# Four residual norms: the first two tiles prepared in token halves, and every residual add moved from GpSimd to VectorE

## The chip, the cores and the metric

The kernel runs on one core of a Trainium2 chip. The metric is the device time of one launch in microseconds (us), lower is better. Engines are named by the profile's short names: PE is TensorE (matmuls), DVE is VectorE, ACT is ScalarE, POOL is GpSimd, SP is the engine whose queue issues the weight loads.

## The reference, cut to what matters

512 tokens of width 1024, all in float32, go through a first block (dilated and stick-breaking attention, cross attention, a gated MLP) and then through a second block of two layers. In that second block every sub-layer ends with a norm of its output that is added onto the residual, and the next sub-layer begins with a norm of the new residual:

```
h = h + 0.5 * rms_norm_2(swiglu(rms_norm_2(h, g[0]), ...), g[1])   # "post" norm g[1] onto h
hn = rms_norm_2(h, g[2])                                           # "pre" norm of the sum
m = gmlp_mixer(hn, ...)            # layer 0;   layer 1: rwkv7_mixer(hn, ...)
h = h + rms_norm_2(m, g[3])
h = h + 0.5 * rms_norm_2(swiglu(rms_norm_2(h, g[4]), ...), g[5])
gate = sigmoid(rms_norm_2(h, g[6]) @ ple_w_gate[i])
h = h + rms_norm_2(gate * (p[i] @ ple_w_proj[i]), g[7])
```

where `rms_norm_2(x, g) = x * rsqrt(mean(x*x) + 1e-6) * g`.

## The kernel before, in words

The residual `h` and the outputs lie feature-major in SBUF: 8 tiles of 128 features x 512 tokens. A matmul in float32 accuracy is made of three products on operands rounded to a shorter type: high x high, high x low and low x high, where high is the rounded value and low the rest. So ACT makes `xh` (high) and DVE makes `xl` (low) of each activation tile, and ACT and DVE split each chunk of weights into `wh` and `wl` (L329 and L345). Weight chunks stream from HBM in a fixed order, two ahead, each issued by SP when the `wl` of the chunk two before is made. Engines run their queues in program order and meet by counting semaphores; no planner is at work, the order is that of the Python text.

The change concerns the class `Deferred`, the stage at the boundary of two sub-layers, where it has a post norm to be added onto `h`. Steps at such a boundary:

1. PE sums the squares of the sub-layer's output (L824), ACT takes the root (L787), DVE the reciprocal (L879), and PE spreads the result over the partitions by four small matmuls into PSUM, one for each block of 128 tokens (L854, in the order 0, 2, 1, 3, with one wait in the middle). PE then multiplies a constant with no use for the result (`keep_busy`, L1000), 5 matmuls long.
2. For each tile t, DVE multiplies the output by gain and scale into a scratch tile (`gained`, L929); the scratch has two buffers. The sum onto `h` is made by DVE for tile 0 (`add_first`, L940) and by POOL for tiles 1 to 7 (`add_on_pool`, L936).
3. For each tile, ACT makes the high part of `h` times the next norm's gain (L1062), and DVE the low part (`low`, L1115). The scale of the next norm is not in it: it is applied to the products later, at the eviction.
4. PE multiplies each tile as it arrives against the first two chunks of weights (`multiply_arriving`): high with `wh` and with `wl` for the first chunk, high with `wh` for the second, then, at tile t, it waits for the low part of tile t itself.
5. Only after its own tiles does DVE split the next weight chunk (L345), add up the 7 squares that ACT makes of `h` (L874), and, ahead of a feed-forward, form sums and differences of `h` (`mixed_first`, `mixed_rest`, L2538 to L2549). PE sums the squares (L817) after three quarters of the second chunk's `wl` products; ACT and DVE make the scale (L883 to L887), PE spreads it (L858) within the third chunk's products.

Boundaries with such a post norm are six. Two of them (class `Beside`, before the gate of the embedding) have other matmuls woven in. The other four lie ahead of the gated mixer's first matmul (`gv`, from 1240 us on) and ahead of three feed-forwards (from 1530, 1947 and 2772 us on). Ahead of the feed-forwards a matmul moves 512 tokens; in `gv` the tokens are the stationary side, 4 blocks of 128, and a matmul has 256 columns of weights.

Of the kernel before, what the change touches and what calls it, by code (L numbers as in the profile page):

```python
# [233 lines left out]
def _build(nc, io, ctx, block):  # L234
# [113 lines left out]
    def linear(name, kt, cols, xs, act_part=None, dve_part=None, steps=(0, 0), halves=False, token_blocks=None,  # L348
# [152 lines left out]
        def _(pe):  # L501
            def multiply(unit, half, m, t, fresh, only=None):


                slot, lot = (a + unit // lots * per + half) % 2, unit % lots
                b, o = bank(unit, m)
                hi, lo = xs(t + half * kt)
                r = last_rows if t == kt - 1 else P
                if token_blocks:
                    wc, xc = slice(t * cols, (t + 1) * cols), slice(token_blocks[m] * P, (token_blocks[m] + 1) * P)  # L510
                    products = [(hi[0:r, xc], wh[0:r, slot, wc]), (hi[0:r, xc], wl[0:r, slot, wc]),
                                (lo[0:r, xc], wh[0:r, slot, wc])]
                    out = ps[:, b, o:o + cols]
                else:
# [4 lines left out]
                    hi, lo = hi[:, tokens], lo[:, tokens]  # L519
                    products = [(wh[0:r, slot, wc], hi[0:r]), (wh[0:r, slot, wc], lo[0:r]),  # L520
                                (wl[0:r, slot, wc], hi[0:r])]
                    out = ps[0:mc, b, 0:hi.shape[-1]]
# [18 lines left out]
            def multiply_arriving():  # L541
# [26 lines left out]
                last.then_inc(chunks_used, 1)  # L568

            def multiply_by_halves(unit, opened):  # L570

# [23 lines left out]
            if paired:  # L595
                multiply_arriving()
                for unit in range(1, in_halves):
                    multiply_by_halves(unit, filled and unit == 1)
# [26 lines left out]
    class Stage:  # L625
# [27 lines left out]
        scaled_late = False  # L653
        tile_by_tile = False

        def sum_pe(self, pe):
# [8 lines left out]
    class Made(Stage):  # L665
# [3 lines left out]
        def __init__(self, per_tile):  # L669
            self.per_tile, self.base = per_tile, dve_steps.base  # L670
# [60 lines left out]
    class Pass:  # L731
# [3 lines left out]
        def __init__(self, number, source, gain, split=None, plain=None, onto=False, tokens=EVERY, by="tensor",  # L735
                     deferred=False, total=None, stat=0):
            self.source, self.gain, self.split, self.plain, self.onto, self.tokens = source, gain, split, plain, onto, tokens
# [14 lines left out]
            for s, n in ((n_square, 0 if by == "before" else KD), (n_add, KD - 1 if by == "vector" else 0),  # L752
                         (n_sum, KD if by == "tensor" else 1), (n_mean, 0 if self.quarters else 1), (n_root, 1),
                         (n_scale, 1 if self.quarters else 2), (n_spread, 4 if self.quarters else 1),
                         (n_value, 0 if deferred else KD), (n_onto, KD if onto else 0), (n_high, KD if split else 0),
                         (n_low, KD if split else 0)):
                self.at[s] = s.total
                s.total += n

        def wait(self, engine, s, step):  # L760

            engine.wait_ge(s.sem, self.at[s] + step)

        def view(self, x):
            return x.rearrange("p (a t) -> p a t", a=2) if self.quarters else x

        def wait_result(self, engine, t):

            self.wait(engine, n_onto if self.onto else n_low if self.split else n_value, t + 1)

# [140 lines left out]
        def dve(self, dve):  # L911
# [10 lines left out]
            self.finish(dve, KD - 1)  # L922

        def gained(self, dve, t):
            if t == 0:
# [7 lines left out]
        def add_on_pool(self, pool, t):  # L933
            self.wait(pool, n_value, t + 1)
            dst = h[:, t, self.tokens]
            nc.gpsimd.tensor_tensor(dst, self.scratch(2 + t % 2), dst, ALU.add).then_inc(n_onto.sem, 1)  # L936
# [65 lines left out]
    class Deferred(Stage):  # L1002

        scaled_late = True
        ahead = None


        def __init__(self, gain, post=None, source=None, split=x_split, tokens=EVERY, keep=None, summed_before=False,
# [6 lines left out]
            self.keep = rs if keep is None else keep  # L1015
            self.post = Pass(0, by="before", **post) if post else None
            self.two = Pass(1, self.source, gain, tokens=tokens, by="before" if summed_before else "vector", deferred=True,
# [3 lines left out]
            self.high_at, self.low_at, self.kept_at = n_high.total, n_low.total, n_kept.total  # L1021
            n_high.total += KD
            n_low.total += KD
# [6 lines left out]
        def split_act(self, act):  # L1030
# [13 lines left out]
            if not self.landed:  # L1044
                self.highs(act, 0, KD)
# [19 lines left out]
        def pe(self, pe):  # L1065
            if self.post:
# [6 lines left out]
                self.post.spread(pe)  # L1073
                keep_busy(pe, 5 if self.post.onto else 3)

# [4 lines left out]
        def split_dve(self, dve):  # L1080
# [8 lines left out]
            if self.post:  # L1089
                self.post.invert(dve)  # L1090
            for t in range(KD):
                if self.post and self.post.onto:
# [12 lines left out]
        def pool(self, pool):  # L1105
            if self.post and self.post.onto:
                for t in range(1, KD):
                    self.post.add_on_pool(pool, t)

        def low(self, dve, t):  # L1110
            if self.post:
                self.post.wait_result(dve, t)
            dve.wait_ge(n_high.sem, self.high_at + t + 1)
            hi, lo = self.split(t)
# [6 lines left out]
        def wait_high(self, pe, t):  # L1121
            pe.wait_ge(n_high.sem, self.high_at + t + 1)

        def squares_dve(self, dve):
# [1972 lines left out]
    class Beside(Deferred):  # L3097

        def __init__(self, gain, post):
            Deferred.__init__(self, gain, post=post)
# [1636 lines left out]
```

## Time and profile before

| | |
|---|---|
| time, median of 3 runs | 3203.94 us (3202.12 to 3207.87) |
| the profiled execution's own time | 3205.45 us |
| its span in the trace | 3203.6 us |
| mean granted PE clock | 0.997 |
| PE busy | 3143.8 us, 98% of the span |
| DVE busy | 2140.0 us, 67% |
| ACT busy | 1481.1 us, 46% |
| POOL busy | 127.4 us, 4% |

Busy time of an engine is the union of its instructions' times. Rows of the timeline below give: start in us from the span's start, duration in us, engine, line of the kernel, operation, output<-inputs, shape, count of instructions merged, and in brackets the idle time of that engine just before, with what ended it.

### The profile page before, as it was taken

To read this page: it belongs to the slowest core of one execution; us is meant where nothing else is said; L and a number is where in the kernel's file an instruction comes from. 1 tells how busy PE (TensorE), PEld (TensorE's weight loads), DVE (VectorE), ACT (ScalarE), POOL (GpSimd) and SP (SyncE) were. 2 spreads that over 40 slices of the span, in tenths; PEclk is the share of its full clock that TensorE was granted. 3 is DMA by queue.
4 is the path that set the end of the run, shared out by engine and by line. 5 is a ranking of instruction groups with operands and counts; after the bars stand their busy time and mean duration, and the time that the engine had idled before them with its cause. 6 is when DMAs were issued, how large, how long until landed. Compare 5 with 4: busy or idle time off the path is not lost. (4 is left out here: it accounts for less than half of the span.)

```text
span 3203.6 us, 54216 instructions
## 1 busy us (share of the span) xinstructions
PE 3143.8 (98%) x22914; PEld 2704.5 (84%) x22914; DVE 2140.0 (67%) x3130; ACT 1481.1 (46%) x2289; POOL 127.4 (4%) x131
## 2 busy tenths in 40 slices
PE   9999999999999999999999999999999999999998
PEld 7887787888889988988899887998777787799986
DVE  6546766775389845363898458996667665799737
ACT  3357644443255523432555345554336564455524
POOL 2100000000000001000100011000110000100002
PEclk9999999999999999999999999999999999999999
DMA  5311232232323323222232332332223000133331
GB/s 184 114 53 66 92 106 79 92 101 90 104 76 108 104 100 113 94 89 92 79 106 98 106 101 72 106 106 100 85 81 103 16 4 16 66 104 108 106 100 65
DMA packets 47249, 287.17 MB, mean 90 GB/s; under 512 B 6416, under 2 KB 6688, under 8 KB 21408
## 3 DMA queue, kind: packets, MB, share of 16 engines
q1 hardware_dynamic: 44960, 279.51, 25.7%
q0 software_dynamic: 2048, 4.20, 0.4%
q8 instruction: 182, 2.98, 0.4%
q14 instruction: 59, 0.48, 0.0%
HBM read 277.39 MB, written 2.10 MB: 87 GB/s over the span
## 5 line engine op out<-in xcount | busy, mean ns | idle before, releaser
L345 DVE TENSOR_TENSOR wl<-raw,wh 128x2048 fp32r<-128x2048 f32 (+3 forms) x211 | 424.8, 2013 | 324.1 <-ACT wh L329 323.6
L528 PE MATMUL ps<-xh,wh 128*128 128x512 f32 (+1 forms) x1312 | 511.4, 396 | 16.0 <-DVE wl L345 4.3
L528 PE MATMUL ps<-xl,wh 128*128 128x512 f32 (+1 forms) x1312 | 486.5, 391 | 0.3
L329 ACT CAST wh<-raw 128x2048 fp32r<-128x2048 f32 (+2 forms) x208 | 348.6, 1676 | 277.4 <-PE ps L528 267.6
L528 PE MATMUL ps<-xh,wl 128*128 128x512 f32 (+1 forms) x1312 | 462.0, 392 | 0.0
L2701 ACT CAST wh<-raw 128x512 fp32r<-128x512 f32 x432 | 262.5, 619 | 230.7 <-DVE raw L2720 114.4
L528 PE MATMUL ps<-hid_h,wh 128*128 128x512 f32 x880 | 342.8, 390 | 0.9 <-DVE wl L345 0.9
L528 PE MATMUL ps<-hid_l,wh 128*128 128x512 f32 x880 | 342.4, 389 | 0.0
L528 PE MATMUL ps<-hid_h,wl 128*128 128x512 f32 x880 | 342.3, 389 | 0.0
L2712 DVE TENSOR_TENSOR wl<-raw,wh 128x512 fp32r<-128x512 f32 x432 | 297.3, 690 | 65.3 <-ACT wh L2701 64.2
L2894 PE MATMUL ps<-mix_h,wh 128*128 128x256 f32 x1152 | 327.0, 284 | 1.3 <-DVE tmp L2831 1.2
L2895 PE MATMUL ps<-mix_l,wh 128*128 128x256 f32 x1152 | 326.0, 283 | 0.0
L2896 PE MATMUL ps<-mix_h,wl 128*128 128x256 f32 x1152 | 325.9, 283 | 0.0
L528 PEld LDWEIGHTS ps<-xh,wh 128*128 128x128 f32 (+1 forms) x1312 | 246.0, 188 | 84.3 <-issue 22.7
L528 PEld LDWEIGHTS ps<-xl,wh 128*128 128x128 f32 (+1 forms) x1312 | 245.6, 188 | 56.4 <-DVE xl L1115 2.9
L528 PEld LDWEIGHTS ps<-xh,wl 128*128 128x128 f32 (+1 forms) x1312 | 245.3, 187 | 53.3 <-issue 1.0
L2896 PE MATMUL ps<-xh,wl 128*128 128x256 f32 x864 | 244.5, 283 | 0.0
L2895 PE MATMUL ps<-xl,wh 128*128 128x256 f32 x864 | 244.5, 283 | 0.0
L2894 PE MATMUL ps<-xh,wh 128*128 128x256 f32 x864 | 244.5, 283 | 0.0
L2894 PEld LDWEIGHTS ps<-mix_h,wh 128*128 128x128 f32 x1152 | 221.1, 192 | 3.1 <-DVE tmp L2831 2.3
L2895 PEld LDWEIGHTS ps<-mix_l,wh 128*128 128x128 f32 x1152 | 221.1, 192 | 0.0
L2896 PEld LDWEIGHTS ps<-mix_h,wl 128*128 128x128 f32 x1152 | 221.1, 192 | 0.0
(537 smaller groups left out, 5918.2 us busy)
## 6 DMA issues: line engine op xcount, KB each, us to landing
raw<-in_up SPq DMA_DIRECT2D x88, 1024.0 KB, 4.9
raw<-in_down SPq DMA_DIRECT2D x64, 704.0 KB, 4.0
raw<-in_up_c SPq DMA_DIRECT2D x22, 1024.0 KB, 4.9
raw<-in_down_c SPq DMA_DIRECT2D x16, 704.0 KB, 4.0
raw<-in_gates SPq DMA_DIRECT2D x8, 1024.0 KB, 5.0
raw<-in_gv SPq DMA_DIRECT2D x8, 1024.0 KB, 4.9
raw<-in_gu SPq DMA_DIRECT2D x8, 1024.0 KB, 5.0
raw<-in_gout SPq DMA_DIRECT2D x8, 1024.0 KB, 4.8
```

Of the source, the lines that this page charges most:

```text
L329: nc.scalar.copy(wh[:, slot, 0:w], raw[:, slot, 0:w]).then_inc(hi_ready, 1)
L345: nc.vector.tensor_tensor(wl[:, slot, 0:w], raw[:, slot, 0:w], wh[:, slot, 0:w].bitcast(F32), ALU.subtract).then_inc(lo_ready, 1)
L528: last = nc.tensor.matmul(out, stationary, moving, start=(fresh and q == 0), stop=(t == kt - 1 and half == per - 1 and q == 2), skip_group ...
L2701: split = nc.scalar.copy(part(wh, u, what), source(u, what))
L2712: split = nc.vector.tensor_tensor(part(wl, u, what), source(u, what), part(wh, u, what).bitcast(F32), ALU.subtract)
L2894: nc.tensor.matmul(out, hi_w[:, at_], hi, start=(fresh and j == 0), stop=False, skip_group_check=True)
L2895: nc.tensor.matmul(out, hi_w[:, at_], lo, start=False, stop=False, skip_group_check=True)
L2896: done = nc.tensor.matmul(out, lo_w[:, at_], hi, start=False, stop=(j == KQ - 1), skip_group_check=True)
```

## The change

Four boundaries (all but the two of class `Beside`, which gets `whole = True`) are given a list `steps`: tile 0 and tile 1 for the first 256 tokens, tile 0 and tile 1 for the second 256 tokens, then tiles 2 to 7 whole. DVE scales and adds, ACT rounds, and PE multiplies in these ten steps. All adds onto `h` are on DVE. PE's order becomes: at tile t the high products of both chunks, then the low products of tile t-1 for both chunks. The spreading matmuls go in the order 0, 1, 2, 3 with two waits among them, and 2 `keep_busy` matmuls follow in place of 5.

```diff
+    def cut(x, part):
+        return x[:, part * (T // 2):(part + 1) * (T // 2)]
...
+            def multiply_arriving_halves():
+                pe.wait_ge(psum_read.sem, psum_read.base - 1)
+                pe.wait_ge(lo_ready, a + 1)
+                for t, part in norms.steps:
...
+                    opening = t == 0 and part == 0
+                    norms.wait_high_step(pe, t, part)
+                    for m in ms:
+                        fresh = opens(0, m, t) if token_blocks else opening
+                        multiply(0, 0, m, t, fresh, "high", part)
+                        multiply(0, 0, m, t, False, "weight_low", part)
...
+                    for m in ms:
+                        multiply(1, 0, m, t, opens(1, m, t) if token_blocks else opening, "high", part)
+                    if part != 0 and t:
+                        norms.wait_tile(pe, t - 1)
+                        for m in range(blocks):
+                            multiply(0, 0, m, t - 1, False, "x_low")
+                            multiply(1, 0, m, t - 1, False, "x_low")
+                norms.wait_tile(pe, kt - 1)
...
-                for n, b in enumerate((0, 2, 1, 3)):
-                    if n == 2:
-                        self.wait(pe, n_spread, 2)
+                for n, b in enumerate(range(TB) if self.halved else (0, 2, 1, 3)):
+                    if n in ((1, 3) if self.halved else (2,)):
+                        self.wait(pe, n_spread, n)
...
+        def gained_half(self, dve, t, part):
+            if t == 0:
+                self.wait(dve, n_spread, 2 + 2 * part)
+            nc.vector.scalar_tensor_tensor(cut(tmp[:, 2 + t, :], part), cut(self.source[:, t, :], part),
+                                           vec[:, self.gain + t:self.gain + t + 1],
+                                           ps[:, 2 + part, P:3 * P], ALU.mult, ALU.mult).then_inc(n_value.sem, 1)
+
+        def add_on_vector(self, dve, t, part):
+            self.wait(dve, n_value, self.done(t, part))
+            old, value = (x if part is None else cut(x, part) for x in (h[:, t, :], tmp[:, 2 + t % 2, :]))
+            nc.vector.tensor_tensor(old, value, old, ALU.add).then_inc(n_onto.sem, 1)
...
-                keep_busy(pe, 5 if self.post.onto else 3)
+                keep_busy(pe, 2 if self.steps else 5 if self.post.onto else 3)
...
+            if self.steps:
+                for t, part in self.steps[:4]:
+                    self.post.gained_half(dve, t, part)
+                    self.post.add_on_vector(dve, t, part)
+                self.post.gained(dve, 2)
+                self.low(dve, 0)
+                self.post.add_on_vector(dve, 2, None)
+                self.low(dve, 1)
+                for t in range(3, KD):
+                    self.post.gained(dve, t)
+                    self.post.add_on_vector(dve, t, None)
+                    self.low(dve, t - 1)
+                self.low(dve, KD - 1)
+                return
...
-                for t in range(1, KD):
+                for t in range(KD if self.steps else 1, KD):
                     self.post.add_on_pool(pool, t)
```

## Rows read from the trace of the kernel before

**Rows 1.** The page, busy time, share of span and instructions of each engine.

```profile
PE 3143.8 (98%) x22914; PEld 2704.5 (84%) x22914; DVE 2140.0 (67%) x3130; ACT 1481.1 (46%) x2289; POOL 127.4 (4%) x131
```

**Rows 2.** Timeline of PE at the boundary from 1947 us on.

```profile
1946.96 1.07 PE L854 MATMUL ps<-sums_p,const 32*128 32x128 f32 x8 [0.17 <-DVE sums_p L879]
1947.96 2.43 PE L1000 MATMUL ps<-const 128*128 128x256 f32 x10
1950.48 0.47 PE L528 MATMUL ps<-xh,wh 128*128 128x512 f32 x1
...
1969.43 2.88 PE L528 MATMUL ps<-xh,wl 128*128 128x512 f32 x12
1972.15 0.94 PE L817 MATMUL ps<-const,rs 128*128 128x1 f32 x8
...
1974.50 0.47 PE L528 MATMUL ps<-xh,wh 128*128 128x512 f32 x1 [0.37 <-ACT wh L329]
...
1977.49 1.12 PE L858 MATMUL ps<-rs,const 128*128 128x512 f32 x2 [0.44 <-DVE rs L887]
```

**Rows 3.** Waits of PE, whole span: us in total, times, longest.

```profile
PE ps L858 <- DVE rs L887: 1.3, 3, 0.5
```

**Rows 4.** Timeline of DVE at the same boundary.

```profile
1948.11 0.75 DVE L929 SCALAR_TENSOR_TENSOR tmp<-proj,vec,ps 128x512 f32<-128x512 f32 x1 [1.20 <-PE ps L854]
1948.89 0.69 DVE L940 TENSOR_TENSOR h<-tmp,h 128x512 f32<-128x512 f32 x1
1949.50 0.74 DVE L929 SCALAR_TENSOR_TENSOR tmp<-proj,vec,ps 128x512 f32<-128x512 f32 x1
...
1960.42 1.12 DVE L1115 SCALAR_TENSOR_TENSOR xl<-h,vec,xh 128x512 fp32r<-128x512 f32 x1
...
1963.56 0.75 DVE L1115 SCALAR_TENSOR_TENSOR xl<-h,vec,xh 128x512 fp32r<-128x512 f32 x1 [0.31 <-ACT xh L1062]
1964.23 2.28 DVE L345 TENSOR_TENSOR wl<-raw,wh 128x2048 fp32r<-128x2048 f32 x1
1966.43 5.46 DVE L874 TENSOR_TENSOR rs<-rs,tmp 128x512 f32<-128x512 f32 x7
...
1972.60 0.48 DVE L2546 SCALAR_TENSOR_TENSOR mix<-h,vec,mix 128x256 f32<-128x256 f32 x1
...
1976.74 0.69 DVE L887 TENSOR_TENSOR rs<-const,stats 128x512 f32<-128x512 f32 x1
```

**Rows 5.** Timeline of ACT at the same boundary.

```profile
1961.03 0.73 ACT L1062 ACTIVATE xh<-h,vec 128x512 fp32r<-128x512 f32 x1 [0.98 <-POOL h L936]
1962.73 0.72 ACT L1062 ACTIVATE xh<-h,vec 128x512 fp32r<-128x512 f32 x1 [0.98 <-POOL h L936]
...
1972.47 1.89 ACT L329 CAST wh<-raw 128x2048 fp32r<-128x2048 f32 x1
```

**Rows 6.** Timeline of POOL at the same boundary.

```profile
1950.32 1.29 POOL L936 TENSOR_TENSOR h<-tmp,h 128x512 f32<-128x512 f32 x1 [46.35 <-DVE tmp L929]
1952.89 9.80 POOL L936 TENSOR_TENSOR h<-tmp,h 128x512 f32<-128x512 f32 x6 [1.28 <-DVE tmp L929]
```

**Rows 7.** Lines L1062 and L3091, 256 columns: duration min/median/max, ns.

```profile
L1062 ACT ACTIVATE mem_h<-mem,vec x8: 496/498/507, 399.7 to 402.5; 128x256 fp32r<-128x256 f32 x8
...
L3091 DVE TENSOR_TENSOR proj<-tmp,proj x4: 418/419/420, 1943.2 to 3185.8; 128x256 f32<-128x256 f32 x4
```

**Rows 8.** Timeline of DVE and PE at the boundary of gv, from 1240 us.

```profile
1258.64 5.46 DVE L874 TENSOR_TENSOR rs<-rs,tmp 128x512 f32<-128x512 f32 x7
...
1262.46 3.04 PE L528 MATMUL ps<-wl,xh 128*128 128x256 f32 x24
...
1265.34 0.95 PE L817 MATMUL ps<-const,rs 128*128 128x1 f32 x8
```

**Rows 9.** Timeline of PE at 2368 us; then by windows (PEclk: third figure from the end).

```profile
2368.04 0.47 PE L528 MATMUL ps<-xh,wh 128*128 128x512 f32 x1 [1.89 <-DVE xl L3635]
...
2350.00:2375.00 25.00, 23.11 (x95) 17.24 (x94) 23.89 (x36) 13.18 (x18) 0.00 (x0) 0.93 0.26 85
```

More of the change, by code:

```diff
@@ L501, in _, with multiply @@
         def _(pe):
-            def multiply(unit, half, m, t, fresh, only=None):
+            def multiply(unit, half, m, t, fresh, only=None, part=None):
                 slot, lot = (a + unit // lots * per + half) % 2, unit % lots
@@ L518, in multiply @@
                     wc = slice(w0, w0 + mc)
-                    hi, lo = hi[:, tokens], lo[:, tokens]
+                    hi, lo = (x[:, tokens] if part is None else cut(x, part) for x in (hi, lo))
                     products = [(wh[0:r, slot, wc], hi[0:r]), (wh[0:r, slot, wc], lo[0:r]),
                                 (wl[0:r, slot, wc], hi[0:r])]
-                    out = ps[0:mc, b, 0:hi.shape[-1]]
+                    out = ps[0:mc, b, 0:tokens.stop - tokens.start] if part is None else cut(ps[0:mc, b, :], part)
                 weight_low = 1 if token_blocks else 2
@@ L568, in multiply_arriving @@
                 last.then_inc(chunks_used, 1)
+            def multiply_arriving_halves():
+                pe.wait_ge(psum_read.sem, psum_read.base - 1)
+                pe.wait_ge(lo_ready, a + 1)
+                for t, part in norms.steps:
+                    if token_blocks:
+                        ms = range(blocks) if part is None else (2 * part, 2 * part + 1)
+                    else:
+                        ms = range(blocks)
+                    opening = t == 0 and part == 0
[4 more added lines that the diff above has]
+                        multiply(0, 0, m, t, False, "weight_low", part)
+                    if opening:
+                        pe.wait_ge(psum_read.sem, psum_read.base)
+                        pe.wait_ge(hi_ready, a + 2)
+                    for m in ms:
[6 more added lines that the diff above has]
+                norms.wait_tile(pe, kt - 1)
+                for m in range(blocks):
+                    last = multiply(0, 0, m, kt - 1, False, "x_low")
+                last.then_inc(chunks_used, 1)
             def multiply_by_halves(unit, opened):
@@ L595, in _ @@
             if paired:
-                multiply_arriving()
+                if norms.steps:
+                    multiply_arriving_halves()
+                else:
+                    multiply_arriving()
                 for unit in range(1, in_halves):
@@ L654, in _build @@
         tile_by_tile = False
+        steps = None
         def sum_pe(self, pe):
@@ L754, in __init__ @@
                          (n_scale, 1 if self.quarters else 2), (n_spread, 4 if self.quarters else 1),
-                         (n_value, 0 if deferred else KD), (n_onto, KD if onto else 0), (n_high, KD if split else 0),
+                         (n_value, 0 if deferred else KD + 2 * halved), (n_onto, KD + 2 * halved if onto else 0),
+                         (n_high, KD if split else 0),
                          (n_low, KD if split else 0)):
@@ L762, in wait, with done @@
             engine.wait_ge(s.sem, self.at[s] + step)
+        def done(self, t, part=None):
+            return t + 3 if self.halved and part != 0 else t + 1
         def view(self, x):
@@ L767, in wait_result @@
         def wait_result(self, engine, t):
-            self.wait(engine, n_onto if self.onto else n_low if self.split else n_value, t + 1)
+            self.wait(engine, n_onto if self.onto else n_low if self.split else n_value, self.done(t))
         def scratch(self, n):
@@ L933, in add_on_pool @@
         def add_on_pool(self, pool, t):
-            self.wait(pool, n_value, t + 1)
+            self.wait(pool, n_value, self.done(t))
             dst = h[:, t, self.tokens]
@@ L1005, in _build @@
         ahead = None
+        whole = False
         def __init__(self, gain, post=None, source=None, split=x_split, tokens=EVERY, keep=None, summed_before=False,
@@ L1015, in __init__ @@
             self.keep = rs if keep is None else keep
-            self.post = Pass(0, by="before", **post) if post else None
+            halved = bool(post and post.get("onto")) and not self.whole
+            if halved:
+                self.steps = [(t, part) for part in range(2) for t in range(2)] + [(t, None) for t in range(2, KD)]
+            self.post = Pass(0, by="before", halved=halved, **post) if post else None
             self.two = Pass(1, self.source, gain, tokens=tokens, by="before" if summed_before else "vector", deferred=True,
@@ L1021, in __init__ @@
             self.high_at, self.low_at, self.kept_at = n_high.total, n_low.total, n_kept.total
-            n_high.total += KD
+            n_high.total += KD + 2 * halved
             n_low.total += KD
@@ L1043, in split_act @@
                 split_hi(act, n, 16 * (n // 2 + 1), n % 2, order[n][2])
-            if not self.landed:
+            if self.steps:
+                for t, part in self.steps:
+                    self.post.wait(act, n_onto, self.post.done(t, part))
+                    high, x = (y if part is None else cut(y, part) for y in (self.split(t)[0], self.source[:, t, :]))
+                    nc.scalar.activation(high, x, ACT.Copy,
+                                         scale=vec[:, self.gain + t:self.gain + t + 1]).then_inc(n_high.sem, 1)
+            elif not self.landed:
                 self.highs(act, 0, KD)
@@ L1090, in split_dve @@
                 self.post.invert(dve)
+            if self.steps:
+                for t, part in self.steps[:4]:
[11 more added lines that the diff above has]
+                return
             for t in range(KD):
@@ L1112, in low @@
                 self.post.wait_result(dve, t)
-            dve.wait_ge(n_high.sem, self.high_at + t + 1)
+            dve.wait_ge(n_high.sem, self.high_at + t + (3 if self.steps else 1))
             hi, lo = self.split(t)
@@ L1122, in wait_high, with wait_high_step @@
             pe.wait_ge(n_high.sem, self.high_at + t + 1)
+        def wait_high_step(self, pe, t, part):
+            pe.wait_ge(n_high.sem, self.high_at + self.post.done(t, part))
         def squares_dve(self, dve):
@@ L3097, in _build @@
     class Beside(Deferred):
+        whole = True
         def __init__(self, gain, post):
```

3 lines of the change are left out of this document (2 added, 1 removed).

## The prediction

> **What bounds the kernel now.** I read the page's busy times first: PE works 98% of the span [rows 1], so only places where PE stands still, or multiplies for nothing, can give time back. Next the timelines of PE, DVE, ACT and POOL side by side at the four changed boundaries; they are alike to a few hundredths, so one stands for all. Three things are to be seen.
>
> First, the front. PE has the scale spread at 1948.03, then multiplies a constant for 2.43 us, and its first real matmul starts at 1950.48 [rows 2]. It waits for the chain gained tile, add, rounding: DVE 0.75 and 0.69 [rows 4], ACT 0.72 [rows 5]. Second, the tiles arrive faster than PE uses them. ACT rounds one every 1.70 us, each time released by POOL [rows 5], whose six adds take 9.80/6 = 1.63 us apiece [rows 6]. PE has ten 512-column matmuls a tile at 0.227 us from start to start (2.72 us for twelve [rows 2]), so 2.27 us a tile. Third, and this decides: behind the tiles DVE runs without a gap, from the next weight chunk's split (1964.23) over the seven adds of squares (from 1966.43, 5.46 us) to the next norm's scale (L887, 1976.74) [rows 4]. PE meets this chain three times: the sum L817 at 1972.15, only 0.26 us after the last add of squares (1971.89), the third chunk at 1974.50 after 0.37 us of waiting, and the spread L858 at 1977.49 after 0.44 us of waiting for L887 [rows 2]. That last wait appears exactly three times in the whole run [rows 3], once before each feed-forward. There DVE is the bound, not PE. Ahead of gv it is not: the adds end at 1264.10 and PE comes to its sum at 1265.34, 1.24 us later [rows 8].
>
> **The change part by part** (times as at the boundary of rows 2).
>
> Spread. Four matmuls with one wait take 1.07 us [rows 2]. DVE now starts after two of them with a wait between. The gain is between nothing and half, 0.53; the wait stays inside the short part, so I take 0.22. DVE's start moves from 1948.11 to 1947.89. The second wait costs at most 0.4 at the end of the spread, and two constant matmuls instead of five take 0.97 instead of 2.43 us [rows 2]: PE is free at about 1949.4, before its data.
>
> Halved tiles. A half on DVE: the gained half 0.48, by the 256-column operation of the same kind [rows 4], and the add 0.42 [rows 7]. Dependent operations follow after 0.03 (0.75 from 1948.11, next at 1948.89), independent ones 0.08 before the last has ended (0.69 from 1948.89, next at 1949.50) [rows 4]. A half step is 0.48+0.03+0.42-0.08 = 0.85, four are 3.40 us; two whole tiles with both adds on DVE would be 2.8. ACT's half is 0.50 [rows 7]. So the first matmul can start at 1947.89+0.48+0.03+0.42+0.04+0.50+0.14 = 1949.50, which is 0.98 earlier.
>
> Adds on DVE. Without POOL beside it the low part falls from 1.12 to 0.75 [rows 4]. A tile now costs DVE (0.74+0.03)+(0.69-0.08)+(0.75-0.08) = 2.05 us, against 1.70 as POOL set the pace. Summed from DVE's start: 3.40; gained 2, low 0, add 2, low 1 = 0.66+0.67+0.61+0.67 = 2.61; five tiles 10.25, of which the last low part must wait for ACT's rounding and starts at 16.54; the weight split follows at 17.21. Before, it was 1964.23-1948.11 = 16.12. DVE is 1.09 later, less the 0.22 of the spread: **0.87 us later** at 1965.10. ACT's last rounding, and with it its squares, moves alike.
>
> PE's new order. Its work is the same 80 matmuls up to the second chunk's `wl` products, 18.14 us. Twelve of them are cut in two ahead of the feed-forwards: 24 of 256 columns at 0.12 (3.04 us for 24 less the last one's tail [rows 8]) against 12 at 0.227, +0.16. Waits: three half steps come 0.13 slower than PE eats them (0.39), 0.08 for the low part of tile 0, 0.45 for tile 2, then none, since 2.05 is under 2.27. PE reaches the `wl` products at 1949.50+18.30+0.92 = 1968.72 instead of 1969.43, and its sum at 1971.44, 0.71 earlier. In gv no matmul is cut, and the same count gives about 0.7 too.
>
> What is late next. DVE's last add of squares now ends at 1971.89+0.87 = 1972.76, so the sum starts at 1972.82: PE stands 1.38 us. Everything that DVE and ACT do next keeps its order: the third chunk's rounding on ACT (1972.47) ends 0.87 later, PE resumes at 1975.37; L887 ends at 1978.30 and the spread starts at 1978.36 instead of 1977.49. PE and the helpers are then 0.87 late together, and nothing later knows an absolute time, so it stays. SP's loads hang on the splits, hence also 0.87 later; a chunk needed at 1979 was asked for before 1968 and has room. Bounds for one feed-forward: -0.7, if DVE's delay were nothing, and +1.5, if each of some ten dependent steps paid 0.06 more. Taken: +0.87, three times = +2.6. In gv the adds end at 1264.10+0.87 = 1264.97, PE's sum starts at 1265.03 instead of 1265.34: -0.3, of the 0.7 that PE had. POOL's 28 adds vanish; nobody else waits for POOL there.
>
> **Sum:** 3 x 0.87 - 0.3 = +2.3 us. Against the profiled execution's 3205.45 (span 3203.6 and 1.85 around it) that is 3207.8; that execution lies 1.5 above the median of the runs, 3203.94, so I give **3206.2**.
>
> One rule speaks against this. POOL's add takes 1.29 us alone and 1.63 in the row of six, DVE's low part 0.75 alone and 1.12 beside it [rows 4, 6]. The Trainium skill (SBUF — State Buffer, "SBUF: two separate sides") says that GpSimd and a VectorE instruction with two SBUF inputs take their shared port as an exclusive lock, held for the whole instruction. By that rule a tile would have cost 1.29+0.75 = 2.04 before, as much as 2.05 now, and the moved adds would be free. The trace disagrees: the period is 1.70, so part of the two ran side by side, and five tiles lose 0.35 each.
>
> **The rivals.**
> (a) PE's gain is kept: DVE's delay is absent or finds slack. For it: the removed contention, and 28 adds whose latency falls from 1.63 to 0.69. Against it: the gap of 0.26 us at L817 and the wait at L858. Each boundary gives 0.7: 3203.94-2.8 = 3201.1. This is also where the rule of the exclusive lock ends.
> (b) Slower by the clock. The new stand of 1.38 us before L817, followed by 128x1 matmuls and a second stand before the third chunk, is near the one stand of 1.89 us after which the granted clock fell: over 25 us it averaged 0.93, so about 1.7 us were lost [rows 9]. It decides if the fall reaches past 1978.36, where PE has no slack left. Three times up to 1.5: 3206.2+4.5 = 3210.7.
> (c) Dependent steps on DVE cost more than I count, since every tile now passes DVE three times in a row: 0.06 more on each, +0.6 a boundary, 3206.2+2.1 = 3208.3.
> (d) The change does not do what it says, the halves being no earlier because all four spread matmuls are in PSUM before DVE can start: start only 0.5 earlier, and the DVE chain later by the 0.22: 3206.9, the forecast in effect.
>
> **How the numbers follow.** Forecast with (d) 0.60, (a) 0.20, (b) 0.08, (c) 0.12. What can be told from no change here is about 0.2%, 6.4 us. Even (a) is far inside it, and its largest form, in which all 1.8 us of PE's front gain and waits vanish at four places, is 7 us: faster 0.04. Slower needs (b) in full on top of the forecast, or (b) with (c): 0.07. Same 0.89. The range takes in (a), (c) and most of (b), plus a microsecond for the medians' own spread (3202.12 to 3207.87): 3200 to 3210; the forecast's own is 3204.5 to 3208.5.
>
> **What would show it.** First real matmul about 1.0 us earlier after the spread than the 2.45 of before. L1115 at 0.75 everywhere in the four stretches and a period of 2.05 between tiles. PE standing before L817 for over 1 us ahead of the feed-forwards, and a little in gv. L858 more than 0.5 us later after DVE's first gained tile than before. It is wrong if L817 comes earlier than before at a feed-forward, if the wait for L887 is gone, or if the granted clock at one of the four places is under 1.

## The result, and the profile after

The changed kernel takes **3209.72 us** (median of 20 runs, 3207.08 to 3214.95) against 3204.22 (20 runs, 3202.12 to 3208.91) for the kernel before: ratio **1.0016, 95% interval 1.001 to 1.0022**, that is 3 to 7 us longer. This is inside the 0.2% that I had called no change; the loss itself is resolved. The forecast was 3206.2 and the range 3200 to 3210. A few executions far longer than the rest of their kernel are left out of the ratios and of the averages of the clock. The profiled execution took 3209.87 us, its span is 3208.1, against 3205.45 and 3203.6 before.

The page's busy times after, to be set against [rows 1]:

```profile
PE 3145.1 (98%) x22926; PEld 2706.2 (84%) x22926; DVE 2145.8 (67%) x3174; ACT 1483.6 (46%) x2297; POOL 82.9 (3%) x103
```

POOL has its 28 adds less and DVE 44 instructions more, yet DVE's busy time rose by only 5.8 us, since its low parts became shorter. The sums say little; the boundary tells more. The timeline of PE after, at the boundary of [rows 2] (start, us, engine, line, operation; in brackets the idle time before it and who ended it):

```profile
1947.52 1.61 PE L898 MATMUL ps<-sums_p,const 32*128 32x128 f32 x8 [0.17 <-DVE sums_p L923]
1949.05 1.13 PE L1056 MATMUL ps<-const 128*128 128x256 f32 x4
1950.20 0.35 PE L532 MATMUL ps<-xh,wh 128*128 128x256 f32 x1
...
1969.48 2.88 PE L532 MATMUL ps<-xh,wl 128*128 128x512 f32 x12
1973.47 1.05 PE L861 MATMUL ps<-const,rs 128*128 128x1 f32 x8 [1.11 <-DVE rs L918]
...
1976.03 0.77 PE L532 MATMUL ps<-xh,wh 128*128 128x512 f32 x1 [0.46 <-ACT wh L333]
...
1979.98 1.02 PE L902 MATMUL ps<-rs,const 128*128 128x512 f32 x2
```

I measure from the scale spread (L854 before, L898 now). The first real matmul comes 2.68 us behind it instead of 3.52; PE reaches the `wl` products (x12) after 21.96 instead of 22.47; but the sum of squares (L817, now L861) starts after 25.95 instead of 25.19, since PE stands for 1.11 us ahead of it. The next norm's spread (L858, now L902) comes 32.46 behind instead of 30.53. DVE shows why (rows that answer to [rows 4]):

```profile
1948.58 0.48 DVE L971 SCALAR_TENSOR_TENSOR tmp<-proj,vec,ps 128x256 f32<-128x256 f32 x1 [1.12 <-PE ps L898]
...
1949.43 0.47 DVE L971 SCALAR_TENSOR_TENSOR tmp<-proj,vec,ps 128x256 f32<-128x256 f32 x1
...
1962.09 0.74 DVE L1195 SCALAR_TENSOR_TENSOR xl<-h,vec,xh 128x512 fp32r<-128x512 f32 x1
...
1964.14 0.74 DVE L1195 SCALAR_TENSOR_TENSOR xl<-h,vec,xh 128x512 fp32r<-128x512 f32 x1
...
1965.75 2.28 DVE L349 TENSOR_TENSOR wl<-raw,wh 128x2048 fp32r<-128x2048 f32 x1
1967.95 5.47 DVE L918 TENSOR_TENSOR rs<-rs,tmp 128x512 f32<-128x512 f32 x7
```

A half step takes 0.85, a tile 2.05 (1964.14-1962.09), and the weight split starts 17.17 behind the first gained tile instead of 16.12. From there on the chain has its old length. Over the whole span, PE's waits at the sum (us in total, times, longest) are new:

```profile
PE ps L861 <- DVE rs L918: 3.6, 4, 1.2
...
PE ps L902 <- DVE rs L931: 0.4, 1, 0.4
```

Four stands make 3.6 us, three of 1.11 to 1.16 and one of 0.17 in gv. The wait for the next scale, three times before [rows 3], is left once. It did not go because DVE got earlier: at the other two feed-forwards PE itself was late, by its clock. By windows (us of the window, busy time of PE, PEld, DVE, ACT, POOL with counts, **granted clock**, DMA share, GB/s):

```profile
1556.00:1560.00 4.00, 4.00 (x12) 2.86 (x12) 3.54 (x11) 3.94 (x5) 0.00 (x0) 0.57 0.02 4
...
1975.00:1980.00 5.00, 4.54 (x14) 3.33 (x13) 4.57 (x11) 4.47 (x6) 0.00 (x0) 0.66 0.00 0
2804.00:2808.00 4.00, 3.09 (x12) 2.11 (x13) 3.57 (x9) 3.91 (x6) 0.00 (x0) 1.00 0.00 0
```

In the first two the granted clock lost 0.43 of 4 us and 0.34 of 5 us, 1.7 us each: it was at the lower of its two levels, 1.2 GHz, for about 3.4 us. In the third it stayed at 2.4 GHz. Before, it stayed there at all four boundaries.

From spread to next spread, us (the boundaries are named for what follows; "sum" is the start of the sum behind the spread):

| | gv | first ff | second ff | third ff | all four | sum at a ff |
|---|---|---|---|---|---|---|
| before | 30.42 | 30.51 | 30.53 | 30.52 | 121.98 | 25.2 |
| after | 30.30 | 31.83 | 32.46 | 31.51 | 126.10 | 26.0 |
| difference | -0.12 | +1.32 | +1.93 | +0.99 | +4.12 | +0.8 |

The third shows a feed-forward without a fall of the clock: +0.99. Three of these and gv make +2.85; the two falls add 0.33 and 0.94. The remaining 0.4 of the span's 4.5 lies elsewhere: -0.56 ahead of the first boundary, +1.85 between the second and third feed-forward, about -0.85 behind the last.

### The profile page after: what moved, and what is told of

Read it like the earlier page. It is cut to its first block and busy times, and to the rows that moved or that the text cites. A ratio compares the mean times of both kernels' runs of the same rounds, so it can differ in the third digit from the quotient of the medians.

```text
span 3208.1 us, 54264 instructions
## 1 busy us (share of the span) xinstructions
PE 3145.1 (98%) x22926; PEld 2706.2 (84%) x22926; DVE 2145.8 (67%) x3174; ACT 1483.6 (46%) x2297; POOL 82.9 (3%) x103
## 5 line engine op out<-in xcount | busy, mean ns | idle before, releaser
L532 PE MATMUL ps<-xh,wh 128*128 128x512 f32 (+3 forms) x1336 | 515.1, 394 | 15.6 <-DVE wl L349 4.1
L532 PEld LDWEIGHTS ps<-xh,wh 128*128 128x128 f32 (+2 forms) x1336 | 250.7, 188 | 84.9 <-issue 21.9
L532 PEld LDWEIGHTS ps<-xh,wl 128*128 128x128 f32 x1324 | 248.0, 188 | 52.9 <-issue 1.0
```

## The experiments

Each edit is shown against the changed kernel, except where another is named. None leaves out any of the computation. "ff" is a feed-forward, "lost clock" the time at 1.2 GHz times one half.

**e1: halves, but tiles 2 to 7 added by GpSimd.**

```diff
-                self.post.gained(dve, 2)
-                self.low(dve, 0)
-                self.post.add_on_vector(dve, 2, None)
-                self.low(dve, 1)
...
+                for t in range(2, KD):
+                    self.post.gained(dve, t)
+                    self.low(dve, t - 2)
+                self.low(dve, KD - 2)
...
-                for t in range(KD if self.steps else 1, KD):
+                for t in range(2 if self.steps else 1, KD):
```

> Halves for tiles 0 and 1 as in the change, but tiles 2 to 7 are added by GpSimd again. Theory (the VectorE chain sets the time ahead of the feed-forwards, and it is the moved adds that lengthen it): VectorE needs 3.4 us for the half steps, then GpSimd sets 1.63 to 1.70 us a tile, so the weight split behind the tiles starts about 15.4 us after the first gained half (16.1 before, 17.2 with the change), the wait for the next scale goes, and the time from the spread of one scale to that of the next falls from 30.5 to about 29.8 us at all four boundaries: about 3 us under the kernel before. Rival (the halves themselves cost, by twice the instructions): that time stays at 31 us or more at the feed-forwards, and the kernel is 1 to 3 us above the one before.

Measured: 3206.26 us against 3204.59, ratio 1.0005, interval 0.9996 to 1.0014. The four boundaries are 30.41, 30.32, 30.32 and 30.30, 0.63 less in all than before. Its PE and DVE at the second feed-forward (spread at 1943.99; DVE from the low part of the fifth tile on):

```profile
1969.19 0.95 PE L861 MATMUL ps<-const,rs 128*128 128x1 f32 x8
1974.31 1.13 PE L902 MATMUL ps<-rs,const 128*128 128x512 f32 x2 [0.43 <-DVE rs L931]
```

```profile
1955.55 1.12 DVE L1191 SCALAR_TENSOR_TENSOR xl<-h,vec,xh 128x512 fp32r<-128x512 f32 x1
...
1957.25 1.12 DVE L1191 SCALAR_TENSOR_TENSOR xl<-h,vec,xh 128x512 fp32r<-128x512 f32 x1
...
1961.05 2.28 DVE L349 TENSOR_TENSOR wl<-raw,wh 128x2048 fp32r<-128x2048 f32 x1
```

With GpSimd's adds back, the low parts take 1.12 again, the period is 1.70, the split comes 16.00 behind the first gained tile, the stand ahead of the sum and the falls of the clock are gone, and the wait for the scale is back at its 0.43. So without the moved adds there is no delay. From the spread to the split the chain is 0.21 shorter than before, and the boundary is 0.20 shorter. But the 0.83 us by which the first matmul is still earlier has come to nothing by the sum (+25.20, as before): PE spends 0.73 of it waiting for the third tile. The 3 us that I expected for this kernel did not come: the split is at 16.00 and not at 15.4.

**e2: no halves; every add on VectorE.**

```diff
-                self.steps = [(t, part) for part in range(2) for t in range(2)] + [(t, None) for t in range(2, KD)]
+                self.steps = [(t, None) for t in range(KD)]
+                halved = False
...
-                for t, part in self.steps[:4]:
-                    self.post.gained_half(dve, t, part)
-                    self.post.add_on_vector(dve, t, part)
+                for t in range(2):
+                    self.post.gained(dve, t)
+                    self.post.add_on_vector(dve, t, None)
```

> No halves (whole tiles, the old order of the spreading matmuls, five matmuls on a constant), all adds on VectorE, TensorE's new order. Theory: 2.05 us a tile on VectorE for all eight tiles, so the weight split starts about 16.6 us after the first gained tile (16.1 before, 17.2 with the change), the next spread is 0.4 to 0.5 us later at three boundaries, TensorE stands 0.6 us before the sum and its granted clock stays at 1.0: about 1.3 us above the kernel before. Rival (all of the loss is the moved adds, none of it the halves): 1.0 us later at three boundaries and the clock falls as with the change, 4 to 5 us above.

Measured: 3206.89 us, ratio 1.0005, interval 0.9997 to 1.0014; boundaries 29.92, 31.81, 30.96, 30.96. PE and DVE at the second feed-forward (spread at 1947.40):

```profile
1972.82 1.05 PE L861 MATMUL ps<-const,rs 128*128 128x1 f32 x8 [0.75 <-DVE rs L918]
1975.37 0.47 PE L532 MATMUL ps<-xh,wh 128*128 128x512 f32 x1 [0.45 <-ACT wh L333]
1978.36 1.12 PE L902 MATMUL ps<-rs,const 128*128 128x512 f32 x2 [0.48 <-DVE rs L931]
```

```profile
1948.55 0.75 DVE L985 SCALAR_TENSOR_TENSOR tmp<-proj,vec,ps 128x512 f32<-128x512 f32 x1 [1.20 <-PE ps L898]
...
1965.10 2.28 DVE L349 TENSOR_TENSOR wl<-raw,wh 128x2048 fp32r<-128x2048 f32 x1
```

The split comes 16.54 behind the first gained tile (16.55 by these rounded rows), 0.42 later than before, and a feed-forward costs +0.44 where the clock holds, not +0.99. In this order the moved adds make 0.42 of the chain's 1.05 and the halves 0.63. The two do not simply add up, though: with GpSimd's adds the halves cost nothing (16.00 in e1 against 16.12), for there GpSimd's pace of 1.70 a tile decides; and on top of the halves the moved adds cost 1.17 (17.17 against 16.00). The halves cost only once DVE sets the pace. At the first feed-forward the clock fell (1.7 us of clock lost) and the boundary took 0.85 more. gv is 0.50 shorter than before, its best here: there nothing waits for DVE.

**e3: the change, and two constant matmuls ahead of the sum at the feed-forwards.**

```diff
+        def sum_pe(self, pe):
+            if self.steps:
+                keep_busy(pe, 2)
+            Deferred.sum_pe(self, pe)
```

> The change, with two matmuls on a constant (0.97 us) ahead of the sum of squares before each feed-forward, where TensorE stands 1.16 us. Theory (part of the loss is the clock, which falls after that stand): the stand shrinks to 0.2 us, the granted clock is 1.0 at all boundaries, spread to spread is 31.5 us at each feed-forward (31.8, 32.5 and 31.5 with the change), 1 to 1.5 us under the change. Rival (the fall of the clock has nothing to do with that stand): it falls as before at one or more of the three, and the time is that of the change.

Measured: 3210.8 us, ratio 1.002, interval 1.0011 to 1.0029. The stand shrinks to 0.29 and the clock holds at two feed-forwards (31.50, 31.49), but falls at the third (32.48). The time is not under the change's. One filling doesn't settle the clock: it fell at 2806.12, after stands of only 0.29 and 0.47. e7 fills more.

**e4: the new order of PE alone** (shown against e2: DVE's loop and GpSimd's adds are those of the kernel before).

```diff
-                for t in range(2):
+                for t in range(KD):
                     self.post.gained(dve, t)
-                    self.post.add_on_vector(dve, t, None)
...
+                    if t == 0:
+                        self.post.add_first(dve)
...
+                    if t >= 3:
+                        self.low(dve, t - 2)
...
-                for t in range(KD if self.steps else 1, KD):
+                for t in range(1, KD):
```

> Only TensorE's new order (low products of tile t-1 for both chunks behind the high products of tile t); VectorE, ScalarE and GpSimd as before, no halves. Theory: VectorE's chain is untouched, so the next spread stays where it was ahead of the feed-forwards (30.5 us after the first), TensorE only stands longer before the sum; up to 0.4 us earlier in gv: 0 to 0.5 us under the kernel before. Rival (TensorE's order is what sets the time): 0.5 us or more at each boundary, 2 us or more under.

Measured: 3205.27 us, ratio 1.0001, interval 0.9992 to 1.001; boundaries 30.63, 30.53, 30.53, 30.52, split 16.11 behind, PE at the `wl` products after 22.7 instead of 22.5. The order is worth nothing either way at the feed-forwards and +0.2 in gv, where PE binds.

**e5: the change, with the next scale ahead of most of the mixes on DVE.**

```diff
-            for j in (0, 1):
+            for j in (0,) if self.steps else (0, 1):
...
+        def scale_dve(self, dve):
+            Deferred.scale_dve(self, dve)
+            if self.steps:
+                self.mixed_first(dve, 1)
+                self.mixed_rest(dve, 1)
+                self.mixed_first(dve, 2)
```

> The change, and ahead of the three feed-forwards VectorE makes the next norm's scale after the first group of sums and differences of h instead of after all of them (ScalarE's root likewise). Theory (with the change VectorE's chain holds TensorE at three points: the sum, the third chunk's rounding by way of ScalarE, and the spread): only the last of the three is freed, so the sum stays 25.96 us after the spread, the wait for the scale (0.44 us) goes, and the next spread comes at 31.05 instead of 31.5 us where the clock holds: about 1.3 us under the change. Rival (the scale's place in the queue is the whole loss): the spread is back at 30.5 us and the time is that of the kernel before.

Measured: 3211.18 us, ratio 1.0021, interval 1.0011 to 1.003; boundaries 30.31, 32.08, 32.42, 31.85. The clock fell at all three feed-forwards, 1.7 us each, so the gain from the earlier scale can't be read at its boundaries. What it costs can: PE has a wait that the change has not, behind each of them:

```profile
PE ps L2988 <- ACT ps L2861: 1.1, 3, 0.4
```

**e6: the change, and two more operations of DVE ahead of the split**, on scratch that nobody reads again.

```diff
+                for n in (2, 3):
+                    nc.vector.tensor_tensor(tmp[:, n, :], tmp[:, n, :], tmp[:, n, :], ALU.mult)
```

> The change, with two more 512-column VectorE instructions (0.61 us each, on scratch tiles, no use for the result) behind the tiles at each of the four boundaries. Theory: VectorE's chain is the bound at all four, so each of them gets 1.2 us longer: 31.5 us from spread to spread in gv and 32.7 ahead of the feed-forwards, and since TensorE then stands 2.4 us before the sum, the granted clock falls at all three, 0.4 to 1 us more at each: 6 to 8 us over the change. Rival (TensorE is the bound and VectorE has room): under 0.5 us at each, 0 to 2 us over the change.

Measured: 3216.72 us, ratio 1.0035, interval 1.0022 to 1.0047, about 7 us over the change; boundaries 31.51, 33.45, 33.07, 33.09, in all 5.0 us over the change's. DVE and PE at the second feed-forward (spread at 1951.02), and PE's clock there:

```profile
1969.25 1.29 DVE L1171 TENSOR_TENSOR tmp<-tmp 128x512 f32<-128x512 f32 x2
1970.46 2.29 DVE L349 TENSOR_TENSOR wl<-raw,wh 128x2048 fp32r<-128x2048 f32 x1
```

```profile
1978.18 1.05 PE L861 MATMUL ps<-const,rs 128*128 128x1 f32 x8 [2.33 <-DVE rs L918]
1984.09 1.02 PE L902 MATMUL ps<-rs,const 128*128 128x512 f32 x2
```

```profile
1978.00:1983.00 5.00, 4.82 (x18) 3.69 (x19) 4.54 (x14) 4.94 (x7) 0.00 (x0) 0.66 0.00 0
```

The split is 1.21 later (18.38 behind), the stand grew from 1.11 to 2.33, and gv, where the clock held, went from 30.30 to 31.51: 1.21 for 1.21, nothing hides a microsecond of this chain there. At the feed-forwards the clock blurs it: +1.62, +0.61 and +1.58. The clock fell at all three feed-forwards, and at none in gv, whose stand was 1.38.

**e7: three fillings** (e3, one constant matmul ahead of the third chunk's unit, and one ahead of the spread).

```diff
+                keep_busy(pe, 2)      # ahead of the sum
...
+                keep_busy(pe, 1)      # ahead of unit 2
...
+                keep_busy(pe, 1, 3)   # ahead of the next spread
```

> The change, with matmuls on a constant in all three stands ahead of each feed-forward: two before the sum of squares, one before the third chunk, one before the spread (0.49 us each). Theory (the clock falls since TensorE stands several times within a few microseconds; filling only the first stand left 0.3, 0.46 and 0.44 us): the granted clock is 1.0 at all three, spread to spread 31.5 to 31.6 us at each, about 1 us under the change. Rival (the clock falls for another reason, or these fillings cost as much as they save): a fall at one or more of the three, or 32 us at each.

Measured: 3210.14 us, ratio 1.0013, interval 1.0004 to 1.0022; boundaries 30.31, 31.50, 31.50, 31.49. PE at the second feed-forward (spread at 1947.46), then the windows:

```profile
1972.11 1.02 PE L1058 MATMUL ps<-const 128*128 128x256 f32 x4
1973.42 1.05 PE L863 MATMUL ps<-const,rs 128*128 128x1 f32 x8 [0.29 <-DVE rs L920]
1975.35 0.59 PE L1058 MATMUL ps<-const 128*128 128x256 f32 x2
1978.33 0.59 PE L1058 MATMUL ps<-const 128*128 128x256 f32 x2
1978.96 1.13 PE L904 MATMUL ps<-rs,const 128*128 128x512 f32 x2
```

```profile
1555.00:1560.00 5.00, 4.71 (x24) 3.81 (x25) 4.57 (x13) 4.95 (x8) 0.00 (x0) 1.00 0.02 3
1975.00:1980.00 5.00, 4.93 (x20) 3.19 (x19) 4.57 (x11) 4.41 (x6) 0.00 (x0) 1.00 0.01 3
2805.00:2810.00 5.00, 4.93 (x19) 3.37 (x19) 4.57 (x9) 4.29 (x8) 0.00 (x0) 1.00 0.01 3
```

With the waits filled but for 0.29 us ahead of the sum and 0.04 ahead of the spread, the clock holds at 2.4 GHz at all three. (It fell elsewhere, from 2307.9 and from 2372.8 on.) This leaves DVE's part alone: +0.99, +0.97 and +0.97, and 1.3 us less over the four boundaries than in the change. The medians (3210.14 and 3209.72) don't resolve 1.3 us, and they show no gain: e7's lies 5.2 us over that of the kernel before, and its boundaries account for 2.8 of it.

**e8: a mixture meant to win.** gv as in e2; the feed-forwards as e1 with e5's early scale, each place so that DVE's chain is not the later one.

```diff
+        by_halves = False     # gv; True where a feed-forward follows
...
+                if self.by_halves:
+                    for t in range(2, KD):
+                        self.post.gained(dve, t)
+                        self.low(dve, t - 2)
```

> Each boundary with what served it best: in gv whole tiles and all adds on VectorE (29.92 us from spread to spread, 30.42 before); ahead of the feed-forwards halves for tiles 0 and 1, GpSimd for tiles 2 to 7, and the early scale. Theory: the wait of 0.43 us for the scale goes from the 30.32 us seen with halves and GpSimd, so 29.9 us at each of the three: 119.6 us over the four against 122.0 before, 2.4 us under the kernel before. Rival (later work on VectorE, moved behind the scale, comes late for the third chunk or the first mixed products): the boundary is 29.9 but TensorE waits as much again later, and the time is that of the kernel before.

Measured: 3208.1 us, ratio 1.0009, interval 1.0 to 1.0019; not faster. Yet its boundaries are 29.92, 29.68, 29.72 and 29.69: 2.97 us less than before. PE's waits over the whole span show where that went:

```profile
PE ps L532 <- DVE hid L2562: 1.9, 3, 0.7
...
PE ps L3005 <- ACT ps L2878: 1.4, 3, 0.5
```

Neither wait is among PE's in the kernel before or the changed one. Each comes once behind each feed-forward boundary, 0.6 and 0.5 us: the mixes that DVE and ACT put off behind the scale reach the feed-forward late. The first lies some ten microseconds behind the spread (1974.92 and 1985.23):

```profile
1974.92 1.02 PE L902 MATMUL ps<-rs,const 128*128 128x512 f32 x2
1985.23 0.50 PE L532 MATMUL ps<-xh,wh 128*128 128x512 f32 x1 [0.63 <-DVE hid L2562]
```

So 2.97 us are gained at the boundaries and 3.3 stood behind them: the early scale moved the wait and did not remove it. That explains no gain; it does not explain the 3 us by which this kernel's median lies above that of the kernel before (3204.97 in these runs). Its profiled execution took 3204.3, but that one is no typical one: its first boundary starts at 1237.01 instead of 1239.16, 2.15 us earlier after a stretch of equal code (e1's likewise, at 1236.46), and the clock did not fall near 2369 (1.7 us), as it did in eight of the ten profiles. With both it would be at about 3208.2, an estimate, close to the median. Where the 3 us lie stays open.

## Why the prediction was right, and where its sizes were off

**The number: inside, by little.** 3209.72 us lies inside the stated range of 3200 to 3210, but only 0.28 us under its top, and outside the forecast's own 3204.5 to 3208.5. It holds because the range had taken in most of rival (b), the clock; in that it is partly luck. Of the three signs that the prediction named for being wrong, two came at two of the three feed-forwards: the wait for the next scale is gone, and the granted clock is under 1. The third, a sum earlier than before, did not come.

**The bound: right.** DVE's chain from the first gained tile over the split and the adds of squares to the next scale sets the end at a feed-forward. Where the clock holds, what the chain gains or loses from spread to split comes out at the next spread: -0.21 and -0.20 in e1, +0.42 and +0.44 in e2, +0.96 and +0.99 in the change; and 1.21 more in e6 makes 1.21 more in gv.

**Spread: 0.22 taken, 0.09 measured.** DVE starts 1.06 behind the spread instead of 1.15. I had bounded the second wait's price and put it at the end of the spread; but the eight records of the spread now take 1.61 us instead of 1.07, and part of that already sits ahead of DVE's start.

**Half steps and tiles: right.** 0.85 forecast and 0.85 measured; 2.05 and 2.05; low part 0.75 and 0.74; split 17.21 and 17.17 behind the first gained tile. With the spread's term, DVE's delay is 1.05-0.09 = 0.96 instead of 0.87. That is the +0.99 of the third feed-forward, less 0.03 at the end. The spread's term alone is 0.13 a place of what the sum lacked.

**PE's front: too large.** The first matmul came 0.83 earlier, not 0.98, and the `wl` products 0.54 (0.51 at the second), not 0.71. At the feed-forwards this costs nothing, since PE stands anyway (1.11 to 1.16, forecast 1.38). It only counts in gv: -0.12, forecast -0.3.

**The clock: the term put at nothing.** This is the step that failed. The forecast has no term for the clock, and rival (b) had a chance of 0.08. In the profiled execution it took place at two of three feed-forwards. I had argued from one stand of 1.89 us [rows 9] and took a stand of 1.38 as still short of that. But a stand of 1.89 us is neither needed nor enough: that same stand near 2368 is in all ten profiles, and the clock fell after it in eight and held in e2 and e8. At the changed boundaries it fell, over all profiled executions, at 0 of 9 feed-forwards where PE stands under 0.5 us at a time from the last tile on (before, e1, e4), at 0 of 3 in e7, where the waits are filled, at 0 of 3 in e8, where PE has no stand ahead of the sum, and at 10 of 15 where it has a stand of 0.29 to 2.33 ahead of the sum and open waits behind it (change 2 of 3, e2 1, e3 1, e5 3, e6 3). Its price was also set wrong: 1.5 a place assumed, 0.33 and 0.94 measured in the change, since most of the 1.7 us of lost clock falls into time in which PE waits for DVE. The Trainium skill ("TensorE: Matmul & The Clock Gate", "A second HAM failure mode: psum-queue depth-cycling") tells of a clock that swings where the engine idles briefly and often between groups of matmuls; the trace agrees in so far as in the changed kernel no stand at these boundaries is above 1.16 us. That it takes several stands is not shown: in six of the ten falls the clock was down before the second stand, or there was no second stand (first feed-forward of the change: the sum at 1555.02 after 1.16 us, the fall from 1556.18 on). I had weighed only the long stand.

**The sum.** +2.3 forecast. By boundaries it is +4.12: 2.85 by DVE's chain and PE's front (against 2.3), and 1.27 by the clock (against 0). The medians say +5.5, with 3 to 7 as the interval, which holds the 4.1. What of 5.5 is above 4.1 stays open. The stretch between the second and third feed-forward takes 793.3 to 798.6 us from one profiled execution to another, in kernels that are equal in it but for what e5 and e8 put off; between e2 and e3 alone that is 5.3 us. Much of that is the clock, by windows in the kernel before and in e2:

```profile
2368.00:2373.00 5.00, 4.96 (x15) 3.95 (x16) 5.00 (x9) 3.06 (x4) 0.00 (x0) 0.66 0.39 162
...
2368.00:2373.00 5.00, 4.07 (x18) 3.39 (x19) 4.91 (x8) 2.80 (x5) 0.00 (x0) 1.00 0.50 197
```

Each fall loses 1.7 us of clock. In this stretch e2 has none (793.3 us); the kernel before, the change, e1 and e4 have one (794.1 to 796.2), e5, e6 and e7 two (796.3 to 798.3), e3 three (798.6). Only e8, with none and 795.7, stands apart, 1.1 of it by its two later waits. So a difference of a few microseconds between two single profiles says little.

The clock's share in a typical execution can be told from the record, for it has the mean granted clock of each, to three places. Time multiplied by one minus the clock, and averaged, is lost clock: 9.1 us before (33 executions, with e1 to e4) and 9.6 (26, with e5 to e8), 13.2 in the change (20), 13.2 in e5 (10), 15.4 in e6 (5), 8.8 in e7 (11). The change loses about 4 us more than the kernel before, as much as 2.4 falls of 1.7 us, so the two falls of its profile are typical; the fillings of e7 take them away. What they cost in time is known from the boundaries alone (1.27), for e7's median is no lower than the change's.

**Rivals (a), (c), (d).** (a) is out: DVE's delay found no slack, as gv in e6 shows. (c), 0.06 more on each dependent step, is out, since steps and tiles took what was forecast. (Its +0.6 a boundary makes +2.4 over four, not the +2.1 given; no chance hung on that.) (d) named a cost of 0.22 that arrived in part (0.13), by another cause than the one named.

**The shared port: the prediction read it too roughly.** By the rule of the exclusive lock, which it took from the Trainium skill (SBUF — State Buffer, "SBUF: two separate sides"), the moved adds would have been free. They are not: e1, with halves and GpSimd's adds, again has a tile every 1.70 us and not every 2.04, and e2, which moves the adds alone, is 0.42 a place later and not equal. But the two do take turns. Single records of the kernel before:

```profile
1955.84 1.74 POOL L936 TENSOR_TENSOR h<-tmp,h 128x512 f32<-128x512 f32 x1
1957.54 1.74 POOL L936 TENSOR_TENSOR h<-tmp,h 128x512 f32<-128x512 f32 x1
...
1957.01 1.12 DVE L1115 SCALAR_TENSOR_TENSOR xl<-h,vec,xh 128x512 fp32r<-128x512 f32 x1
```

The first add ends at 1957.58; the low part, begun during it, ends 0.55 later, at 1958.13; the second add, begun during the low part, ends 1.15 after that, at 1959.28. 0.55+1.15 is the period of 1.70. Wherever the two meet in the kernel before, in e1 and in e4, these distances are the same: 0.54 to 0.56 in 122 cases and 1.14 to 1.16 in 94. The one that starts first keeps its own time: the add of 1.29 at 1950.32 stretches a low part to 1.71, and in e1 a low part of 0.75 at 1949.12 stretches the add begun at 1949.28 to 1.74. So only the first 0.20 of the low part (0.75-0.55) and 0.14 of the add (1.29-1.15) run beside the other, and these 0.34 are what lies between 2.04 and 1.70. The trace agrees with the rule in that one waits for the other, and differs in that this is not for the whole instruction. The prediction's "side by side" is true of 0.34 us only; its price of 0.35 a tile stands.

**What is shown and what is argued.** Shown: the moved adds (0.42 alone) and, on top of them, the halves (0.63) make DVE's delay; it passes to PE one to one where the clock holds; the change loses about 4 us more clock than the kernel before, and with PE's waits filled it does not; e8's gain at the boundaries comes back as two later waits. Argued only: that the clock costs a typical execution the 1.27 us that it costs the profiled one; and that the stand ahead of the sum, which is new, is what makes the clock fall. Equal stands are followed by a fall in one place and not in another, so something is at work that these runs do not vary. Open: what of the medians' +5.5 is not in the +2.85 of the chain, since filling the waits did not bring the median down.

## What to carry to other kernels

Before taking work off a "slow" engine, find which chain binds: here GpSimd took 1.74 us for an add and VectorE 0.69, and the move still lost, because a tile cost the pair 1.70 us as they took turns, and costs VectorE alone 2.05 now that the adds stand in the chain that binds. Feeding the consumer earlier pays only as far as the next thing it waits for; follow both the consumer and the chain to the next two meetings and price the difference there. And when a change opens a stand of a microsecond on TensorE, price the clock as well, with the cover that the remaining waits give. Before two single profiles are set against each other over a long stretch, count the falls of the clock in it.

## What was not expected of the hardware

- The granted clock fell to 1.2 GHz for about 3.4 us behind a stand of 1.1 us and eight 128x1 matmuls, at two feed-forwards of three, and not behind the 0.37 and 0.44 of before. In gv it held even with a stand of 1.38 (e6), and after the same stand of 1.9 near 2368 it held in e2 and e8 and fell in the other eight profiles. With constant matmuls in each wait it held at all three feed-forwards (e7); with one wait filled it fell at one of three (e3).
- GpSimd's add and VectorE's low part wait for each other for all but 0.34 us of the two: a low part ends 0.55 us after the add before it, the add 1.15 us after the low part.
- Putting two waits instead of one into a spread of four small matmuls took its records from 1.07 to 1.61 us.
- Half the columns is far from half the time on DVE: 0.47 against 0.74 for the gained tile, so a tile's two operations take 1.70 us in halves (2 x 0.85) and 1.39 whole (1948.55 to 1949.94 in e2). Two tiles of that make 0.62, the 0.63 of the halves within rounding.
